# Three splits one slot later, an exponential table loaded ahead, and the last turn of a group in another bank

## The reference

```python
# attention, each head and each of three dilations; queries of 128 against their window
s = einsum(q, k) * Dh ** -0.5 - slope * distance          # masked
p = exp(s - max(s)); o = (p @ v) / sum(p)                 # mixed over dilations by denominators

# state-space mixer, chunks of 128 tokens, four groups of eight heads, per chunk:
acum = cumsum(dt * A)
decay = exp(where(causal, acum[l] - acum[s], -inf))
y = (C B^T * decay) @ (x * dt) + (C @ state) * exp(acum)
state = state * exp(acum[-1]) + B^T @ (x * dt * exp(acum[-1] - acum))
# then, on all tokens of a group:
y = (y + D * x) * silu(z);  y = rms(y) * y_g;  out += y @ w_out
```

## Time and profile before

| what | value |
|---|---|
| time, median of 3 runs | 3327.12 us (3324.29 to 3329.75) |
| profiled execution, its own time | 3331.93 us |
| its span, first to last instruction | 3330.4 us |
| granted TensorE clock, mean | 0.967 of 2.4 GHz |
| PE busy | 3112.3 us (93%) |
| PE weight loads busy | 2601.6 us (78%) |
| DVE busy | 1831.2 us (55%) |
| ACT busy | 1394.0 us (42%) |
| POOL busy | 682.2 us (20%) |
| attention | about 564 to 1165 us of the span |
| state-space stage | about 1461 to 2272 us |

### The profile page before, as it was taken

One profiled execution on the slowest core, in us unless ns is written; L12 is line 12 of the kernel. 1 busy time (PEld: TensorE's weight loads), 2 busy tenths in 40 slices (PEclk: granted clock), 3 DMA queues, 4 the chain that ended last, 5 costly groups with the idle time before them and its releaser, 6 DMA issues. The chain is left out here.

```text
span 3330.4 us, 41838 instructions
## 1 busy us (share of the span) xinstructions
PE 3112.3 (93%) x15516; PEld 2601.6 (78%) x15516; DVE 1831.2 (55%) x2485; ACT 1394.0 (42%) x2093; POOL 682.2 (20%) x455
## 2 busy tenths in 40 slices
PE   6999999999999999779999999998899999997799
PEld 5788887888888887657787877776778888886677
DVE  4344222666666533356757666576357777776343
ACT  4333212555555422234334242343246666666331
POOL 3100002222222200211001020010234444443110
PEclk9999999999999999879999999998999999998899
DMA  2111222121111223102111121211111111111321
GB/s 98 41 50 42 70 76 64 58 64 58 51 58 57 93 103 139 33 27 74 48 58 64 45 83 39 70 51 57 69 53 41 43 39 39 39 39 45 120 71 55
DMA packets 55763, 201.69 MB, mean 61 GB/s; under 512 B 6432, under 2 KB 9376, under 8 KB 55328
## 3 DMA queue, kind: packets, MB, share of 16 engines
q1 hardware_dynamic: 46176, 166.76, 15.2%
q0 software_dynamic: 9408, 32.51, 3.1%
HBM read 167.66 MB, written 23.20 MB: 57 GB/s over the span
## 5 line engine op out<-in xcount | busy, mean ns | idle before, releaser
L114 ACT ACTIVATE whi<-wraw 128x1024 fp32r<-128x1024 f32 x208 | 218.4, 1051 | 452.4 <-PE out_D L127 67.6
L119 DVE TENSOR_TENSOR wlo<-wraw,whi 128x1024 fp32r<-128x1024 f32 x173 | 232.8, 1345 | 154.7 <-ACT whi L114 151.1
L125 PE MATMUL ssm_D<-x1hi,whi 128*128 128x512 f32 x640 | 260.2, 407 | 4.4 <-DVEq L1792 4.4
L125 PE MATMUL b_D<-x1hi,whi 128*128 128x512 f32 x640 | 256.0, 400 | 8.5 <-DVEq L1002 6.6
L127 PE MATMUL ssm_D<-x1hi,wlo 128*128 128x512 f32 x640 | 253.3, 396 | 0.0
L126 PE MATMUL ssm_D<-x1lo,whi 128*128 128x512 f32 x640 | 252.8, 395 | 0.0
L126 PE MATMUL b_D<-x1lo,whi 128*128 128x512 f32 x640 | 251.2, 392 | 0.0
L127 PE MATMUL b_D<-x1hi,wlo 128*128 128x512 f32 x640 | 251.0, 392 | 0.0
L2232 DVE TENSOR_TENSOR_SCAN stick_keep<-stick_keep 128x896 f32<-128x896 f32 (+7 forms) x128 | 215.7, 1686 | 43.4 <-ACT stick_keep L2140 42.1
L2371 POOL TENSOR_TENSOR stick_rows<-stick_rows,stick_keep 128x896 f32<-128x896 f32 (+7 forms) x128 | 162.5, 1272 | 272.6 <-DVE stick_keep L2232 272.3
L125 PE MATMUL stick_D<-x1hi,whi 128*128 128x512 f32 x512 | 210.6, 411 | 8.1 <-DVE x1lo L152 8.1
(11 more groups left out here) (413 smaller groups left out, 7982.1 us busy)
## 6 DMA issues: line engine op xcount, KB each, us to landing
wraw<-w_dram SPq DMA_DIRECT2D x208, 512.0 KB, 3.6
sq<-acum_rows SPq DMA_DIRECT2D x32, 512.0 KB, 3.7
att_bias<-alibi_dram SPq DMA_DIRECT2D x16, 512.0 KB, 3.6
stack<-stack POOLq DMA_DIRECT2D x32, 256.0 KB, 3.7
x_sb<-xT_dram SPq DMA_DIRECT2D x8, 512.0 KB, 8.6
branch_a<-sq POOLq DMA_DIRECT2D x8, 512.0 KB, 3.5
y_b<-att_y POOLq DMA_DIRECT2D x8, 512.0 KB, 3.0
f<-y_b SPq DMA_DIRECT2D x2, 2048.0 KB, 8.7
```

Of the source, the lines that this page charges most:

```text
L114: act.activation(self.whi[:, s, :, :], self.wraw[:, s, :, :], ACT.Copy).then_inc(self.w_hi, 1)
L119: dve.tensor_tensor(self.wlo[:, s, :, :], self.wraw[:, s, :, :], self.whi[:, s, :, :].bitcast(F32), ALU.subtract).then_inc(self.w_lo, 1)
L125: pe.matmul(out, self.whi[:, s, w0, :], xhi[:, k, cols], start=start, stop=False)
```

## The change

In the attention, ACT copies the high parts of the next pair's keys one slot later (slot 6 in place of 5); the queries' copies stay. In the state-space stage, DVE's splits of tiles 8, 9 and 10 go one slot later, behind that slot's skip: to slots 1, 5 and 8. ACT gets an exponential of one column into a scratch tile `warm` in slot 0, behind the copy of CB and ahead of the wait for the mask. The last turn-out of a group (chunk 7) writes the bank pX in place of pT, and the last skip reads it there; so turn_out(7) waits for skip(5) in place of skip(6).

```diff
--- before.py
+++ after.py
@@ -880,9 +880,10 @@
                         if slot == half_done_slot(1, 1) + 1:
                             split(p + 1, 3)
                         if more:
-                            for c in (TK, TQ):
-                                if slot == half_done_slot(c, 1) + 1:
-                                    high(p + 1, 1 - q, c)
+                            if slot == half_done_slot(TK, 1) + 2:
+                                high(p + 1, 1 - q, TK)
+                            if slot == half_done_slot(TQ, 1) + 1:
+                                high(p + 1, 1 - q, TQ)
                         if slot == half_done_slot(2, 1) + 1:
                             split(p + 2, 0)
                         if more and slot == 18:
@@ -1399,6 +1400,7 @@
         cb = sb("cb", [P, 2, 2, P])
         state, decayed = sb("state", [P, GC]), sb("decayed", [P, GC])
         y_sb = sb("y_sb", [P, GC])
+        warm = sb("warm", [P, 1])
         u = K.sq
         E = [K.sq[:, s, :].rearrange("p (h l) -> p h l", h=GH) for s in range(2)]
         x_dt, x_dte = [t[:, 0:GC] for t in (K.acc[:, :], xd_odd)], [t[:, GC:2 * GC] for t in (K.acc[:, :], xd_odd)]
@@ -1418,6 +1420,10 @@
         Rg = K.acc
 
         STEPS = NC - 1
+
+        def y_bank(c):
+
+            return pT if c < NC - 1 else pX
 
         def heads(t, c, g, width):
 
@@ -1501,9 +1507,9 @@
 
                 def turn_out(g, c):
                     pe.wait_ge(y_done, 8 * g + (c + 2))
-                    pe.wait_ge(y_turned, 8 * g + (c + 1))
+                    pe.wait_ge(y_turned, 8 * g + min(c + 1, NC - 1))
                     for k in range(GT):
-                        last = pe.transpose(pT[:, k * P:k * P + P], y_sb[:, k * P:k * P + P], K.ident[:, :])
+                        last = pe.transpose(y_bank(c)[:, k * P:k * P + P], y_sb[:, k * P:k * P + P], K.ident[:, :])
                     last.then_inc(s3, 1)
 
                 def group(g):
@@ -1599,6 +1605,8 @@
                                 act.wait_ge(s2, 8 * g + (c - 1))
                             act.activation(cb[:, c % 2, :, :], pCB[:, 0:2 * P].rearrange("p (a b) -> p a b", a=2),
                                            ACT.Copy).then_inc(cb_copy, 1)
+                            if c == 0:
+                                act.activation(warm[:, :], K.eps[:, :], ACT.Exp)
                             act.wait_ge(sel, 8 * g + (c + 1))
                             for h in range(GH):
                                 last = act.activation(E[c % 2][:, h, :], E[c % 2][:, h, :], ACT.Exp,
@@ -1696,7 +1704,7 @@
                     for k in range(GT):
                         last = dve.scalar_tensor_tensor(xs[:, k, cols], xs[:, k, cols],
                                                         K.vec[:, bass.ds(4 * g + (VEC["d_skip"] + k), 1)],
-                                                        pT[:, k * P:k * P + P], ALU.mult, ALU.add)
+                                                        y_bank(c)[:, k * P:k * P + P], ALU.mult, ALU.add)
                     last.then_inc(y_turned, 1)
 
                 def group(g):
@@ -1727,7 +1735,7 @@
                     scale_z(0)
                     block_work(g, 0)
                     weigh(g, 0)
-                    q = Z_FIRST
+                    q, due = Z_FIRST, 0
                     for slot in range(10):
                         if 1 <= slot <= 8:
                             if slot < 8:
@@ -1744,8 +1752,9 @@
                             dve.wait_ge(y_turned, 8 * g + 7)
                             for k in range(GT - 1):
                                 gate_y(k, slice(0, Y_EARLY)).then_inc(yz_early, 1)
-                        if q // 16 > q_old // 16:
-                            split(g, 7 + q // 16)
+                        if due:
+                            split(g, due)
+                        due = 7 + q // 16 if q // 16 > q_old // 16 else 0
                         if slot == 8:
                             for k in range(GT - 1):
                                 dve.wait_ge(y_hi_early, 3 * g + (k + 1))
```

## The result

| | before | changed | ratio |
|---|---|---|---|
| time, median of four runs | 3328.43 us | 3356.51 us | 1.0083 (1.0069 to 1.0098) |
| span of the profiled execution | 3330.4 us | 3352.0 us | |
| granted TensorE clock, mean | 0.967 | 0.963 | |

The changed kernel is slower by 28.1 us. The forecast was slower by 15.4, 3342.5 us with a range to 3354.0: the direction is right, the size is not, and the measured time lies above the range. All ratios here are of fast runs; two of the twelve executions of nobank, 3869 and 7863 us, are not among them.

The account below looks back on a forecast made before the run. TensorE, busy 93%, bounds the kernel, so only its waits count. Per group -0.6 - 0.35 + 4.4 + 1.4 - 1.0 = +3.85 us, times four +15.4, attention 0: from the median 3327.12 to 3342.5 us, range 3330 to 3354.

Parts of the forecast that it names:

- The hold of row 6: Slot 5: tile 9's later split holds SP's load and row 6 behind it, delaying products(6): +4.4 us a group.
- Rival (a): At products(6): row 6's delay is covered and only gains stay, about 3316 us; chance 0.09.
- The clock behind the hole: After PE's stand before products(6): granted clock falls to 0.50 for 3.4 us, +1.4 us a group, 1.7 at most.
- Rival (d): Three DMAs land late, a second low-clock stretch follows, the last turn wins nothing: +29 us, 3356; chance 0.07.
- The table: Head of each group, slot 0: table load moves ahead of the mask wait, exponentials start earlier, -0.6 us a group.
- Tile 8: Slot 1: later split frees DVE, PE's wait before the turn-in goes, products(1) come earlier: -0.35 us a group.
- The third step: From products(1) to products(5) in each group: no change forecast, 0 us.
- The last turn: Chunk 7's turn-out into pX starts earlier, tile 10's split comes later: -1.0 us a group, bounds 0 and -1.9.
- The keys: Attention: keys' high copies one slot later on ACT, low weights still covered, cost 0, bounds +3 and -3 us.

Follow-up runs that it names:

- nobank: Kernel before with the early one-column exponential, splits of tiles 8 and 9 one slot on, row 6 issued ahead of the load: 3325.33 us, ratio 0.9994.
- undo9: Changed kernel with the split of tile 9 back in slot 4: 3326.96 us, ratio 0.9995.
- rowfirst: Changed kernel with only SP's order altered, row 6 issued before the load that waits for tile 9's split: 3324.50 us, ratio 0.9996.
- only9: Kernel before with the split of tile 9 alone one slot later: 3357.81 us, ratio 1.0091.
- fill: Changed kernel with 16 unused products of 512 columns just ahead of products(6)'s wait: 3345.51 us, ratio 1.0061.
- bank: Kernel before with only the last turn's bank changed, pX in place of pT: 3330.48 us, ratio 1.0013.
- keys: Kernel before with the keys' high parts alone one slot later: 3328.65 us, ratio 1.0009.
- behind: Changed kernel with 16 more products of 512 columns behind products(6)'s wait, ahead of the short ones: 3369.20 us, ratio 1.0122.
- fill8: Changed kernel with 8 more products of 512 columns ahead of products(6)'s wait: 3355.35 us, ratio 1.0088.

## Why the prediction was right or wrong

**The hold of row 6: right.** This was the main term, +4.4, and it measured +4.66. Its steps stand in the trace as put: the split behind skip(3), the load half a microsecond later, the row 0.60 behind it, 4.57 us from issue to mask (4.79 assumed), 5.06 from mask to PE (5.0). undo9, rowfirst and only9 show the cause from three sides. Rival (a), that the delay is covered, is refuted with it.

**The clock behind the hole: the step that failed.** The forecast had +1.4 and 1.7 at most, "half of 3.4", because the low stretch behind the last turn lasts 3.4 us. It measured +3.78, and fill takes it away. Two things were taken over from one case to another without a reason: that the stretch has the same length behind a hole twice as long, and that what follows is alike. Behind the last turn come dense products at once. Behind the new hole come 16 products of 64 columns, which took 3.68 us in place of 2.00. Then come 12 dense ones, still at the low clock. With 3.78 for 1.4 the sum would have been +6.23 a group, 24.9 in all, 3352, inside the range; the other 0.75 a group is the row (+0.26), tile 8 (+0.23) and what follows the sums (+0.53), less 0.23 won more at the table. The range was too narrow because this bound was none: the trace of before has low stretches of 6.8 and 10.2 us as well, in other stages, and I had not asked what stood ahead of those. Rival (d) had a second low stretch at 1.3 us, and still as the unlikely end. Its 3356 meets the measured time, but by luck: it took 5.5 for the row (4.66), 2.6 for the clock (3.78), and nothing for the last turn.

**The table: right.** -0.6 forecast, -0.83 measured; the exponential of one column costs less (0.11 us of pitch against 0.25).

**Tile 8: mis-sized.** -0.35 forecast, -0.12 measured. The wait before the turn-in is gone, but weigh(1) took 1.65 us in place of 1.24. The earlier state lets POOL finish the decayed state and make its next mask earlier, at 1548.72, and so ahead of that weighing and beside it:

```profile
1548.72 1.09 POOL L1821 TENSOR_SCALAR_AFFINE_SELECT sq<-sq 128x1024 f32<-128x1024 f32 x1 [2.63 <-DMA sq<-acum_rows]
...
1549.24 1.65 DVE L1677 TENSOR_TENSOR sq<-sq,ssm_cb 128x1024 f32<-128x1024 f32 x1 [3.80 <-ACT sq L1612]
```

In the kernel before the two also ran side by side, but the weighing started 0.11 us ahead, and it was the mask that took long:

```profile
1551.75 1.24 DVE L1669 TENSOR_TENSOR sq<-sq,ssm_cb 128x1024 f32<-128x1024 f32 x1 [0.50 <-ACT sq L1604]
1551.86 2.08 POOL L1812 TENSOR_SCALAR_AFFINE_SELECT sq<-sq 128x1024 f32<-128x1024 f32 x1
```

So who starts first decides. In the four groups of the changed kernel weigh(1) took 1.65, 1.31, 1.53 and 1.22 us, and the step was 0.10, -0.23, -0.01 and -0.33: where the weighing stayed short, the forecast was met. The third step, from products(1) to products(5), scatters by up to 1.2 us a group in either direction for the same cause. Its four weighings together changed by 0.7, -0.7, 1.5 and -0.1 us against before, the step by 0.37, -0.94, 1.17 and -0.37.

**The last turn: the number right to the sums, the account not, and wrong behind them.** -1.0 forecast, -1.09 measured at the sums. The forecast took DVE's stand of 1.88 us before its scale as what could be won, less 0.6. But that stand is itself the delay by the low stretch: where the stretch stayed away, DVE stood 0.21 to 0.24 us with the last turn as it was. -1.09 is -1.63 for the missing stretch and +0.54 for the late split; that all four groups of before have the stretch is luck. The forecast also let the gain run on to the next group. With bank alone it does not: a low stretch comes behind the sums in its four groups, and the time is not better. What brings it is only in part told. In all traces it follows in 18 of the 32 groups with the last turn in pX, where PE stands 0.74 to 0.80 us before the sums, and in none of the 24 with a wait of 0.16 to 0.18. So that wait goes with it but doesn't suffice: rowfirst has the same wait in all groups and the stretch in the third alone.

```profile
1626.50:1629.90 3.40, 3.40 (x19) 1.00 0.00 0
2025.10:2028.50 3.40, 3.40 (x11) 0.51 0.00 0
```

Why the times of undo9 and rowfirst have little to show for the 5.6 and 7.6 us that their single traces win in the stage stays open. A part of it may be that the trace of before is a dear one: four stretches behind the last turn, where the others have 11 in 20 groups. By my estimate that is 4 x 0.45 x 1.6, or 3 us.

**The keys: right within what can be told**, 0 forecast, 0.1 us from the first to the last product of the attention in the trace of keys. In the changed kernel's own trace that stretch is 1.6 us shorter than before (587.7), with the same waits and one low stretch less.

## What to carry to other kernels

Before a step that signals a semaphore is moved, look for who waits for it on each queue, the DMA issuer's above all, and what is queued behind that wait: here one load of weights, itself in no hurry, held a transfer that was. If PE will stand longer than it did anywhere in the stage, don't take the length of a low-clock stretch from a shorter hole; price it by the products that follow it at half speed, and let the upper bound be several such stretches. Count such stretches over several traces before you price one: the same wait in the same program had one behind it in some groups and none in others. A wait may cost nothing but the low stretch behind it, and when it goes, another may come at the next weak place, so a part is worth what a timed run of it alone says.

## What the runs showed of the hardware

- Behind a hole of about 4.4 us the granted clock was 0.50 for 6.8 to 10.2 us when products of 64 columns followed (the changed kernel, only9), and for 3.4 to 6.8 us when products of 512 columns followed (behind). Behind holes of 2.2 to 2.5 us (fill8) it was none, 3.4, 6.8 and 6.8 us. 16 products of 64 columns took 3.68 us at the low clock and 2.00 at the full one, so even these short ones pay nearly double.
- With PE kept at work through the hole by products that nobody needs (fill), no low stretch followed there in any of the four groups.
- Behind the same wait of 1.97 to 2.00 us the clock was low for 3.4 us in 15 of 24 groups and at full in 9. The low stretch costs 1.6 us at the sums, the wait by itself nothing.
- DVE's weighing and POOL's mask, both of 128x1024, slow each other by who starts first. In the trace of before, a weighing with no mask beside it took 1.22 to 1.23 us (12 of them). Where the weighing started first, it took 1.22 to 1.24 and the mask 1.75 to 2.10 (11). Where the mask started first, it took 1.09 and the weighing 1.74 to 2.13 (9).
- A table load of 1.28 us ahead of a wait, and a one-column exponential of 0.20 us, cost ACT the 0.11 us of the latter's pitch and nothing more. That alone is the one version here whose interval lies below before: 3320.56 us, ratio 0.9988 (0.9979 to 0.9997). With twelve such intervals one may do so by chance; the 0.7 to 0.9 us at each products(0) are seen in the trace.
